# Sums over 0/1 matrices as two fp32r matmuls, of a high and a low part, in a two-block transformer kernel

## The reference

```python
# first block: q and k are normed per head of 64; 8 heads, 512 features
q = rms_norm(q.reshape(b, s, ATTN_HEADS, HEAD_DIM), q_g)   # q / sqrt(mean(q*q) + eps)
k = rms_norm(k.reshape(b, s, ATTN_HEADS, HEAD_DIM), k_g)
# second block, stick-breaking attention, 4 heads of 128, keys in chunks of 128
ln = jnp.where(before, jax.nn.log_sigmoid(-z), 0.0)
within = jnp.einsum('bhqcj,ji->bhqci', lnc, tri_within)    # 0/1 matrix, j > i
tot = jnp.sum(lnc, axis=-1)
after = jnp.einsum('bhqc,cd->bhqd', tot, (cidx[:, None] > cidx[None, :]))
logw = z + lnc + within + after
```

## Time and profile before

| | |
|---|---|
| median of 3 runs | 2933.48 us (2933.28 to 2933.89) |
| the profiled execution | 2933.4 us, span 2931.4 us |
| PE busy | 2918.3 us of the span |
| DVE, ACT busy | 1924.0 us, 1511.1 us |
| POOL busy | 239.6 us |
| granted TensorE clock | 1.0 in all slices |

### The profile page before, as it was taken

One profiled execution on the slowest core, in us unless ns is written; L12 is line 12 of the kernel. 1 busy time (PEld: TensorE's weight loads), 2 busy tenths in 40 slices (PEclk: granted clock), 3 DMA queues, 4 the chain that ended last, 5 costly groups with the idle time before them and its releaser, 6 DMA issues. The chain is left out here.

```text
span 2931.4 us, 48844 instructions
## 1 busy us (share of the span) xinstructions
PE 2918.3 (100%) x17288; PEld 2570.4 (88%) x17288; DVE 1924.0 (66%) x2206; ACT 1511.1 (52%) x1896; POOL 239.6 (8%) x199
## 2 busy tenths in 40 slices
PE   9999999999999999999999999999999999999999
PEld 7888898998888888888888888988888888888888
DVE  7696765567665656656655666655787567757775
ACT  5576644454544444444544446555665455545564
POOL 3010020102101010000200000001000000010021
PEclk9999999999999999999999999999999999999999
DMA  8566667665655666556565555556565666666555
GB/s 244 165 184 185 173 182 224 184 180 188 199 187 186 193 189 191 188 184 194 179 198 182 166 160 169 186 184 208 160 202 179 200 187 186 191 188 187 185 159 172
DMA packets 543862, 545.94 MB, mean 186 GB/s; under 512 B 17304, under 2 KB 542112, under 8 KB 543744
## 3 DMA queue, kind: packets, MB, share of 16 engines
q1 hardware_dynamic: 540576, 536.79, 59.7%
q0 software_dynamic: 2480, 7.10, 0.9%
q10 hardware_dynamic: 688, 0.53, 0.1%
HBM read 542.25 MB, written 2.11 MB: 186 GB/s over the span
## 5 line engine op out<-in xcount | busy, mean ns | idle before, releaser
L1648 DVE TENSOR_TENSOR w_low<-raw,w_high 128x1024 fp32r<-128x1024 f32 x1012 | 1261.6, 1260 | 777.6 <-ACT w_high L1082 772.5
L1082 ACT CAST w_high<-raw 128x1024 fp32r<-128x1024 f32 x1012 | 1050.0, 1048 | 996.7 <-PE ps_gemm L704 961.5
L699 PE MATMUL ps_gemm<-act_a,w_high 128*128 128x512 f32 x4448 | 1434.0, 395 | 6.1 <-DVE act_a L1879 2.0
L699 PE MATMUL ps_gemm<-act_b,w_high 128*128 128x512 f32 x3208 | 1044.3, 395 | 0.0
L704 PEld LDWEIGHTS ps_gemm<-act_a,w_low 128*128 128x128 f32 x4608 | 861.7, 188 | 152.0
L704 PE MATMUL ps_gemm<-act_a,w_low 128*128 128x256 f32 x4608 | 991.7, 279 | 0.0
L704 PE MATMUL ps_gemm<-act_b,w_low 128*128 128x256 f32 x3520 | 778.8, 279 | 0.0
L699 PEld LDWEIGHTS ps_gemm<-act_a,w_high 128*128 128x128 f32 x4448 | 713.2, 188 | 53.2 <-issue 7.2
L704 PEld LDWEIGHTS ps_gemm<-act_b,w_low 128*128 128x128 f32 x3520 | 652.5, 189 | 96.9
L699 PEld LDWEIGHTS ps_gemm<-act_b,w_high 128*128 128x128 f32 x3208 | 524.4, 188 | 42.4
L1718 DVE TENSOR_TENSOR summ<-ps_gemm,bcopy 128x512 f32<-128x512 f32 x220 | 150.4, 684 | 8.8 <-ACT bcopy L1097 8.8
(11 more groups left out here) (287 smaller groups left out, 1217.8 us busy)
## 6 DMA issues: line engine op xcount, KB each, us to landing
raw<-in_w_in SPq DMA_DIRECT2D x348, 512.0 KB, 4.2
raw<-in_w_up SPq DMA_DIRECT2D x176, 512.0 KB, 3.5
raw<-in_w_mlp_up SPq DMA_DIRECT2D x128, 512.0 KB, 3.9
raw<-in_w_mlp_down SPq DMA_DIRECT2D x128, 512.0 KB, 3.5
raw<-in_w_down SPq DMA_DIRECT2D x88, 512.0 KB, 3.5
raw<-in_w_out SPq DMA_DIRECT2D x64, 512.0 KB, 4.6
raw<-in_w_branch SPq DMA_DIRECT2D x32, 512.0 KB, 3.7
raw<-in_w_ple_gate SPq DMA_DIRECT2D x32, 512.0 KB, 3.5
```

The lines of the kernel that those rows point to most:

```text
L699: nc.tensor.matmul(ps[:, g, t, :], wh[:, at, o:o + P], x, start=first, stop=False, skip_group_check=True)
L1082: nc.scalar.copy(wh[:, at, :], raw[:, at, :]).then_inc(high_ready, 1)
L1648: nc.vector.tensor_tensor(wl[:, at, :], raw[:, at, :], wh[:, at, :].bitcast(F32), ALU.subtract).then_inc(split_done, 1)
```

## The change

The squares of the first three tiles and the suffix sums are split in the same manner as the weights, and each product with a 0/1 matrix is done twice in fp32r, once over the high part and once over the low part, into the same accumulator. The 0/1 matrices are copied into fp32r tiles: `zo_head`, and later `zo_ones` and `zo_later`, in `wf_s`, which is otherwise unused by then. The fourth tile's squares keep the fp32 product, since their place in `act_b` is needed for results.

On ScalarE a cast to `sq_high` is added after the second square, chained to it; a cast to `l_high` is added after the logarithm, behind a wait for VectorE's `s_ln`. On VectorE the subtraction that makes `sq_low` stands between the first and the second piece of the former `take(fill, 2)`; the one that makes `l_low` stands before `take(fill, 2)`. TensorE waits for `at_low` and `s_low`, which VectorE's subtractions set.

```diff
+        zo_head, zo_ones, zo_later = wf_s[:, 0:P], wf_s[:, 0:P], wf_s[:, P:2 * P]
+        sq_high, sq_low = act_b[:, 15, :], act_b[:, 14, :]
+        l_high, l_low = act_a[:, 12, 0:3 * P], act_a[:, 13, 0:3 * P]
@@ TensorE, first attention @@
                 take(fill, 2)
-                pe.wait_ge(at_sq, c + 1)
+                if c == 0:
+                    pe.wait_ge(zero_one, 1)
+                if c < 3:
+                    pe.wait_ge(at_low, c + 1)
+                else:
+                    pe.wait_ge(at_sq, c + 1)
                 if c:
                     pe.wait_ge(y_high, 12 + c)
-                nc.tensor.matmul(pm[:, 0, :], same_head, G[:, 16:18, :].rearrange("p o n -> p (o n)"),
-                                 start=True, stop=True).then_inc(at_ssq, 1)
+                if c < 3:
+                    nc.tensor.matmul(pm[:, 0, :], zo_head, sq_high, start=True, stop=False)
+                    nc.tensor.matmul(pm[:, 0, :], zo_head, sq_low, start=False, stop=True).then_inc(at_ssq, 1)
+                else:
+                    nc.tensor.matmul(pm[:, 0, :], same_head, G[:, 16:18, :].rearrange("p o n -> p (o n)"),
+                                     start=True, stop=True).then_inc(at_ssq, 1)
@@ TensorE, stick-breaking @@
-                pe.wait_ge(s_ln, h + 1)
-                nc.tensor.matmul(pm[:, 1, 0:S], later, PJ[:, 22, :], start=True, stop=False, ...)
-                nc.tensor.matmul(pm[:, 1, P:S], ones, PJ[:, 23, 0:P], start=False, stop=True, ...)
-                nc.tensor.matmul(pm[:, 1, S:S + P], later, PJ[:, 23, 0:P], start=True, stop=True, ...)
+                if h == 0:
+                    pe.wait_ge(zero_one, 2)
+                pe.wait_ge(s_low, h + 1)
+                nc.tensor.matmul(pm[:, 1, 0:S], zo_later, l_high[:, 0:S], ...)
+                nc.tensor.matmul(pm[:, 1, 0:S], zo_later, l_low[:, 0:S], ...)
+                nc.tensor.matmul(pm[:, 1, P:S], zo_ones, l_high[:, S:3 * P], ...)
+                nc.tensor.matmul(pm[:, 1, P:S], zo_ones, l_low[:, S:3 * P], ...)
+                nc.tensor.matmul(pm[:, 1, S:S + P], zo_later, l_high[:, S:3 * P], ...)
+                nc.tensor.matmul(pm[:, 1, S:S + P], zo_later, l_low[:, S:3 * P], ...)
@@ ScalarE, first attention @@
+                if c == 0:
+                    act.wait_ge(f_logits, 1)
+                    nc.scalar.copy(zo_head, same_head).then_inc(zero_one, 1)
                 nc.scalar.activation(G[:, 16, :], PJ[:, 20 + c, :], ACT.Square)
-                nc.scalar.activation(G[:, 17, :], PJ[:, 24 + c, :], ACT.Square).then_inc(at_sq, 1)
+                if c < 3:
+                    link(nc.scalar.activation(G[:, 17, :], PJ[:, 24 + c, :], ACT.Square))
+                    nc.scalar.copy(sq_high, G[:, 16:18, :].rearrange("p o n -> p (o n)")).then_inc(at_sq, 1)
+                else:
+                    nc.scalar.activation(G[:, 17, :], PJ[:, 24 + c, :], ACT.Square).then_inc(at_sq, 1)
                 take(fill, 2)
@@ ScalarE, stick-breaking @@
                 nc.scalar.activation(l3, l3, ACT.Ln, bias=1.0).then_inc(s_lnb, 1)
+                if h == 0:
+                    act.wait_ge(in_c2, 16)
+                    nc.scalar.copy(zo_ones, ones)
+                    nc.scalar.copy(zo_later, later).then_inc(zero_one, 1)
+                act.wait_ge(s_ln, h + 1)
+                nc.scalar.copy(l_high, l3).then_inc(s_high, 1)
                 take(fill, 3)
@@ VectorE, first attention @@
                 dve.wait_ge(y_done, 12 + c)
-                take(fill, 2)
+                take(fill, 1)
+                if c < 3:
+                    dve.wait_ge(at_sq, c + 1)
+                    nc.vector.tensor_tensor(sq_low, G[:, 16:18, :].rearrange("p o n -> p (o n)"),
+                                            sq_high.bitcast(F32), ALU.subtract).then_inc(at_low, 1)
+                take(fill, 1)
                 dve.wait_ge(at_vps, c + 1)
@@ VectorE, stick-breaking @@
                 link(nc.vector.tensor_tensor(z3[:, S:3 * P], z3[:, S:3 * P], before_neg[:, 0:P], ALU.add))
+                dve.wait_ge(s_high, h + 1)
+                nc.vector.tensor_tensor(l_low, l3, l_high.bitcast(F32), ALU.subtract).then_inc(s_low, 1)
                 take(fill, 2)
```

More of the change, by code:

```diff
@@ L338, in build @@
         sc_z, sc_base, sc_y = sem("sc_z"), sem("sc_base"), sem("sc_y")
+        at_low, s_high, s_low, zero_one = sem("at_low"), sem("s_high"), sem("s_low"), sem("zero_one")
         at_sq, at_ssq, at_rms, at_qk, at_vps, at_v = (
@@ L1002, in _ @@
                 take(fill, 3)
-                pe.wait_ge(s_ln, h + 1)
-                nc.tensor.matmul(pm[:, 1, 0:S], later, PJ[:, 22, :], start=True, stop=False,
+                if h == 0:
+                    pe.wait_ge(zero_one, 2)
+                pe.wait_ge(s_low, h + 1)
+                nc.tensor.matmul(pm[:, 1, 0:S], zo_later, l_high[:, 0:S], start=True, stop=False,
                                  skip_group_check=True)
-                nc.tensor.matmul(pm[:, 1, P:S], ones, PJ[:, 23, 0:P], start=False, stop=True,
+                nc.tensor.matmul(pm[:, 1, 0:S], zo_later, l_low[:, 0:S], start=False, stop=False,
                                  skip_group_check=True)
-                nc.tensor.matmul(pm[:, 1, S:S + P], later, PJ[:, 23, 0:P], start=True, stop=True,
+                nc.tensor.matmul(pm[:, 1, P:S], zo_ones, l_high[:, S:3 * P], start=False, stop=False,
+                                 skip_group_check=True)
+                nc.tensor.matmul(pm[:, 1, P:S], zo_ones, l_low[:, S:3 * P], start=False, stop=True,
+                                 skip_group_check=True)
+                nc.tensor.matmul(pm[:, 1, S:S + P], zo_later, l_high[:, S:3 * P], start=True, stop=False,
+                                 skip_group_check=True)
+                nc.tensor.matmul(pm[:, 1, S:S + P], zo_later, l_low[:, S:3 * P], start=False, stop=True,
                                  skip_group_check=True).then_inc(s_suf, 1)
```

## The result

The changed kernel takes 2943.56 us (median of 8, 2941.13 to 2947.46), the kernel before, beside it, 2934.14 us (2933.28 to 2935.52). The ratio is 1.0033, 95% interval 1.0023 to 1.0042: 0.33% slower, 9.4 us. The profiled execution is one of the shorter ones, 2941.4 us with a span of 2939.4: 8.0 us more than the profiled one of before.

What follows compares the result with a forecast made beforehand. The prediction took TensorE's stream as the bound, so any new wait costs its full length. Stalls 9.1 minus savings 1.2 (squares) and 0.7 (suffix) gave +7.2 us: 2940.7 us, 0.25% slower, range 2938.7 to 2943.6.

Steps and rivals of the forecast that it cites:

- the clock: Rival, chance 0.08: TensorE falls to half speed after the three new stalls, adding 3 x 2.7 = 8.1 us, giving 2948.8.
- Stalls: Squares of tiles 0, 1, 2: TensorE waits for VectorE's subtraction 3.1, 3.0 and 3.0 us, 9.1 in all.
- paid back: Rival, chance 0.06: weight pieces fill during the squares' stalls, TensorE then runs faster; only savings remain, -1.9 us, 2931.6.
- Savings on the squares: Squares of three tiles: two fp32r products take 0.47 instead of 0.86 us, saving 0.39 each, 1.17 in all.
- Suffix sums: Suffix sums of four heads: 0.70 instead of 0.87 us a head, saving 0.17 each, 0.7 us in all.
- the rival at the fp32 price: Suffix sums, chance 0.33: narrow fp32r products cost 0.22 each like fp32, four heads lose 1.0 us, giving 2942.4.
- The cover in front of them: Before the suffix products: low part ready 1.3 us early, next piece 0.8 us early, so zero stall.
- the 1.8 us wait of the earlier trace: Longest TensorE wait in the profile before; it left the granted clock at full, held against the clock rival.
- granted clock 1.0 behind each gap: Sign expected in the profile after: TensorE keeps full clock behind each of the three stalls of about 3 us.
- the forecast's base: Time of the kernel before that the sum started from: profiled execution 2933.4 us, median of the runs 2933.5.
- the narrow products: Rival, chance 0.33: the suffix sums' fp32r products under 256 columns cost the fp32 price, 0.22 us each; 2942.4.
- six slow products in the first microseconds: Program start: six fp32 half products fill 5.4 us instead of 2.7, read as half speed after rest, losing 2.7 us.

Runs made afterwards that it cites:

- e2: Against the changed kernel: VectorE subtracts (sq_low) before both weight pieces instead of between them; median 2938.66 us, profiled execution at full clock 2935.84 us.
- e3: Against the changed kernel: VectorE subtracts after both weight pieces instead of between them; 2950.83 us.
- e10: Against the changed kernel: TensorE takes three pieces before the squares' products and five behind the transposes, VectorE's order unchanged; 2932.93 us, ratio 0.9996 to the kernel before.
- e4: Against the changed kernel: VectorE subtracts before both pieces, and TensorE takes three pieces before the squares' products, five behind the transposes; 2931.76 us.
- e6: The kernel of e2 again without edit, for a trace with the clock down; 2937.55 us.
- e7: Against the changed kernel: the changes at the squares taken out, only the suffix sums split; 2934.05 us, ratio 0.9998 to the kernel before.
- e11: The kernel of e2 again without edit, a third trace; 2937.89 us.
- e12: The kernel of e2 again without edit, a fourth trace; 2938.67 us.
- e1: The changed kernel again without edit, beside the kernel before; 2943.98 us, ratio 1.0034.

## Why the prediction was right and where it failed

The direction and the waits were right: slower, by a wait of TensorE for VectorE at three tiles. The time, 2943.6, is 2.9 us above the forecast and at the very end of the range; measured again it was 2944.0, outside. What failed is the clock, which the sum put at nothing.

**Stalls.** Forecast 3.1, 3.0, 3.0, measured 3.2, 3.0, 3.0, with the releaser, the order and the causes as worked out: VectorE's backlog at tile 0, ScalarE's cast ahead of the weight cast at tiles 1 and 2. e2, e3 and e10 move them as the same reckoning says (to 2.0 and 0.9, to 4.3, to 0.4 and 0.2). They are not paid back: at full clock the groups behind a wait take 0.79 and then 0.71 (from 211.21 in the profile after), and the difference stays to the end. That rival is out.

**Savings on the squares.** Forecast 0.39 a tile, measured 0.31: behind an idle array the first of the pair takes 0.31 to 0.35 to the next start, not 0.23. In e4, with no idle time, the first takes 0.23.

**Suffix sums.** Forecast 0.70 a head, measured 0.68; the rival at the fp32 price, to which I gave 0.33, is out. The fp32r product of 128 columns starts 0.06 to 0.12 apart. The cover in front of them held: no new wait. The mean of the four is 0.10, below the 0.11 that the prediction took as the lower bound. The 81 ns of the Trainium skill ("TensorE: Matmul & The Clock Gate", section "Back-to-back issue gap") is not reached, and the head is as the rows said.

**The clock: the step that failed.** The prediction put it as a rival with 0.08, all or nothing, three times 2.7 us, and held against it that the 1.8 us wait of the earlier trace rows had left the granted clock at full. So the sum has no term for it, and "granted clock 1.0 behind each gap" was the sign that failed. The reading of the earlier trace rows was true of one execution. Of 55 executions of the kernel before that ran beside the experiments, 25 show a mean clock of 0.999 and take 1.3 us longer by the median (2935.2 against 2933.8). The traces of e6, e7, e10, e11 and e12, which all have that wait, have a half-speed stretch behind it; in the other nine it left the clock at full. In steps of 10 us over all 14 traces the granted clock is below full only behind this wait, behind the waits at the squares, and at the very end, after TensorE's last products. That the long executions of the kernel before come from the same wait is the likely reading, but the two traces of that kernel both ran at full clock.

So the forecast's base was itself the shorter of two groups, and behind the new waits the clock falls in a part of the cases: the changed kernel's 13 executions reach from 2941.1, no fall, to 2947.5, which is 6.3 more and so about four stretches of 1.3 to 1.6, as many as it has places where a trace here shows a fall. At 3.0 us of wait I have both in one execution (e1: down after the first, up after the others), at 4.1 us down at all three tiles of the trace and for longer. The 9.4 between the medians is then some 7.9 at full clock (2941.4, the four executions at 1.000, against the 2933.5 that the prediction started from) and 1.5 for falls beyond those that the kernel before has too. The 2.9 above the forecast add up in the same way: 0.6 in the base (2934.1 instead of 2933.5), 0.1 more of stall, 0.2 less of saving, 0.5 from ahead of the squares, and 1.5 for the clock. That the total still stood at the end of the range is luck: the range was made for other things, the narrow products above all.

The price was off too. The 2.7 us came from six slow products in the first microseconds, for which the profile gives a granted clock of 1.00; no run shows that they are slow by the clock. A fall behind a wait cost 1.3 to 1.6 us (2.3 behind the 4.1 us wait). The Trainium skill, "TensorE: Matmul & The Clock Gate", section "Why this matters for your kernels", asks for no gaps over about 3 us in mid kernel; the runs here have falls after gaps of 1.8 and 1.9 us, so the measurement is stricter than the page.

What decides in which execution a given gap brings the clock down stays open. By the mean clocks the same 1.8 us wait did so in up to 25 of 55 executions of the kernel before and in at most two of 11 of e4's. The clock is down before the wait is over in e1 and e3, and only from 0.4 to 1.4 us after it in the seven other traces with such a stretch (e6 to e12); no run here was made to tell why.

The saving that was meant was there, 1.7 us, and it was more than undone, since the product was made cheaper on the engine that was full by putting two more steps, on two other engines, directly ahead of it. With TensorE asking one piece later and VectorE subtracting first, the same products give 2931.76.

## What to carry to other kernels

When an engine that is always busy gets a new wait, find where the engine it now waits for stands in its own queue at that moment; being less busy on the whole doesn't mean being on time there. Place the question after as much independent work as the chain needs (here one piece of 2.8 us), before shaving the work behind it. Look at the clock of many executions, not of the profiled one, before reckoning that a short idle time costs only itself.

## What the runs showed of the hardware that I had not expected

- TensorE at 1.2 GHz (granted clock 0.50) behind idle times of 1.8 to 3.0 us in part of the executions, costing 1.3 to 1.6 us each time on top of the wait; behind 4.1 us at all three tiles of the trace, costing 2.3 at the first. In e12 the half speed at tile 0 began 0.7 us after work had resumed, in e10 behind the norm 1.4 us after; in e1 and e3 the clock was down before the first product.
- Four fp32r products of 128 columns in a row start 0.06, 0.11, 0.11 and 0.12 us before what follows them, 0.10 on the mean.
- At full clock, the first fp32r product of 512 columns behind a wait takes 0.31 to 0.35 us to the next start, and 0.23 in a stream.
